# Linear-time mixers in a two-block network: three sets of block copies, a spread setup, a late norm factor and the low weights last

## The reference

```python
def rms_norm(x, g):
    y = xf * lax.rsqrt(jnp.mean(xf * xf, axis=-1, keepdims=True) + EPS)
    return (y * g.astype(jnp.float32)).astype(x.dtype)
...
def _s5_mixer(h, w_in, log_dt, lambda_re, lambda_im, b_re, b_im, c_re, c_im, d_skip, w_glu, w_out):
    u, z = jnp.split(h @ w_in, 2, axis=-1)
...
    y = jax.nn.gelu(y.reshape(bsz, seq, SSM_WIDTH)).astype(h.dtype)
    ga, gb = jnp.split(y @ w_glu, 2, axis=-1)
    y = ga * jax.nn.sigmoid(gb)
    y = y * jax.nn.silu(z)
    return y @ w_out
...
def odd_mixer(hn, w_in, w_alpha, b_alpha, out_gain, w_out):
    g_q, g_k, g_v, g_r, g_a = jnp.split(hn @ w_in, cuts, axis=-1)
    log_alpha = jax.nn.log_sigmoid((g_a @ w_alpha + b_alpha).astype(jnp.float32)) / GLA_GATE_TAU
    o = gla_chunked(to_heads(g_q, GLA_HEADS), to_heads(g_k, GLA_HEADS),
                    to_heads(g_v, GLA_HEADS), to_heads(log_alpha, GLA_HEADS))
    return (from_heads(rms_norm(o, out_gain)) * jax.nn.silu(g_r)) @ w_out
```

## Time and profile before

| | us |
|---|---|
| median of 3 timed runs | 2016.17 |
| lowest and highest | 2016.15 and 2018.51 |
| the profiled execution | 2015.85 |
| its span (first to last instruction) | 2014.1 |

### The profile page before, as it was taken

How to read it: one execution, slowest core, us unless ns; L and a number is a source line. 1 busy time by engine, 2 the same in 40 slices (tenths; PEclk the granted TensorE clock), 3 DMA queues, 4 the chain that set the end, 5 groups by cost and what they waited for, 6 DMA issues and landing times.

```text
span 2014.1 us, 26711 instructions
## 1 busy us (share of the span) xinstructions
PE 1951.5 (97%) x9866; PEld 1522.2 (76%) x9866; DVE 1121.8 (56%) x2055; ACT 582.2 (29%) x1124; POOL 799.9 (40%) x460
## 2 busy tenths in 40 slices
PE   8999999997999999999899999998999999999999
PEld 5867777776878776667678888886688778888887
DVE  5679998775974545765654445222533464454311
ACT  3136566314641134443321111001323221111100
POOL 3632222375754432222234444443233344444443
PEclk9999999998999999999999999999999999999999
DMA  5611010222212231111122222323121122222232
GB/s 183 184 63 43 33 43 33 85 65 67 69 64 94 88 127 44 62 55 61 53 96 94 94 102 96 100 99 107 53 74 63 65 94 94 99 99 94 100 119 74
DMA packets 55300, 167.66 MB, mean 83 GB/s; under 512 B 8080, under 2 KB 16144, under 8 KB 54816
## 3 DMA queue, kind: packets, MB, share of 16 engines
q1 hardware_dynamic: 47904, 155.22, 22.8%
q10 hardware_dynamic: 7296, 11.09, 2.0%
HBM read 157.90 MB, written 2.10 MB: 79 GB/s over the span
## 4 chain that ended last, share of the span: by engine, by line
issue 42%; PE 32%; POOL 17%; DVE 7%; SPq 1%; POOLq 0%; ACT 0%; DMA 0%; ACTq 0%; DVEq 0%
POOL wlo L167 16%; PE bank L184 6%; PE bank L185 6%; PE bank L186 6%; DVE prob L1620 2%; DVE ssb L1607 2%; SPq L149 1%; PE bank L1242 1%; PE bank L1267 1%; PE bank L935 1%; PE bank L554 1%; PE bank L937 1%; PE bank L936 1%; PE bank L556 1%; PE bank L555 1%
## 5 line engine op out<-in xcount | busy, mean ns | idle before, releaser
L167 POOL TENSOR_TENSOR wlo<-raw,whi 128x1024 fp32r<-128x1024 f32 x248 | 596.8, 2407 | 946.0 <-DVE whi L175 946.0
L175 DVE CAST whi<-raw 128x1024 fp32r<-128x1024 f32 x288 | 206.8, 718 | 408.7 <-PE bank L186 217.8
L184 PE MATMUL bank<-xh,whi 128*128 128x512 f32 x704 | 275.2, 391 | 3.9 <-POOL wlo L155 3.9
L185 PE MATMUL bank<-xl,whi 128*128 128x512 f32 x704 | 274.5, 390 | 0.0
L186 PE MATMUL bank<-xh,wlo 128*128 128x512 f32 x704 | 274.5, 390 | 0.0
L554 PE MATMUL bank<-xh,whi 128*128 128x512 f32 x424 | 177.6, 419 | 1.5 <-POOL wlo L167 1.5
L556 PE MATMUL bank<-xh,wlo 128*128 128x512 f32 x424 | 166.4, 392 | 0.0
L555 PE MATMUL bank<-xl,whi 128*128 128x512 f32 x424 | 165.6, 391 | 0.0
L184 PEld LDWEIGHTS bank<-xh,whi 128*128 128x128 f32 x704 | 132.5, 188 | 32.7 <-POOL wlo L155 5.2
L186 PEld LDWEIGHTS bank<-xh,wlo 128*128 128x128 f32 x704 | 132.6, 188 | 27.8
L185 PEld LDWEIGHTS bank<-xl,whi 128*128 128x128 f32 x704 | 132.6, 188 | 27.3
(11 more groups left out here) (396 smaller groups left out, 3858.9 us busy)
## 6 DMA issues: line engine op xcount, KB each, us to landing
raw<-in_weights_dram SPq DMA_DIRECT2D x288, 512.0 KB, 3.2
h<-in_x_dram SPq DMA_DIRECT2D x2, 1024.0 KB, 7.1
sz<-su SPq DMA_DIRECT2D x128, 16.0 KB, 1.8
out_dram<-h ACTq DMA_DIRECT2D x4, 512.0 KB, 2.6
etab<-in_even_tables_dram ACTq DMA_DIRECT2D x1, 1730.0 KB, 6.5
x_kh<-kvc_h ACTq DMA_DIRECT2D x2, 256.0 KB, 5.1
x_kl<-kvc_l ACTq DMA_DIRECT2D x2, 256.0 KB, 6.9
x_vh<-kvc_h ACTq DMA_DIRECT2D x2, 256.0 KB, 5.0
```

The source lines that it names most:

```text
L167: nc.gpsimd.tensor_tensor(wlo[:, s % 2, :], raw[:, s, :], whi[:, s % 2, :].bitcast(F32), ALU.subtract).then_inc(w_lo, 1)
L175: nc.vector.tensor_copy(whi[:, t_of_4 % 2, :], raw[:, t_of_4, :]).then_inc(w_hi, 1)
L184: nc.tensor.matmul(to, w_h, pe_h, start=first and k == 0, stop=False)
L185: nc.tensor.matmul(to, w_h, pe_l, start=False, stop=False)
```

## The change

It has four parts.

1. In a product tile TensorE waits for `whi` alone, does the 16 matmuls with `whi`, then waits for `wlo` and does the 8 with `wlo`. The helpers that interleave a tile with attention work in quarters (6 matmuls each) do the same in theirs. The two first tiles of each output projection (`pe_out_chunk`), the first two of `glu` and the compression loop stay in the old order.
2. The block copies of `su` are issued in three sets of 16 for the groups 0, 1 to 3 and 4 to 7, instead of eight sets: 48 DMAs instead of 128, of the same bytes in all. Tile 52 is issued behind the first set, 53 to 55 behind the second, none behind the third.
3. Pool's tables are spread over five tiles, `ta` and `tb` in turn, and it no longer fills constants: VectorE does that in six operations behind input tile 4.
4. `N_MIX1` joins `UNSCALED`: `xh` and `xl` come out of `down0`'s residual, the gates use `h` with a `wga` that VectorE scaled by the gain at the end of `up0`, and the square sums run behind the last gate. `rstd` is multiplied in by VectorE where `gas`, the values and the output gates leave their banks (ScalarE took those before) and, for queries and keys, through the exponents (`oe`, four slots instead of three). The tables are loaded at the start of `up0`.

Besides, the square sums in `nsa_kv` come one chunk earlier. The diff, cut to its core; the other product helpers change as `product` does:

```diff
-                for j in range(KC):
-                    sp_blocks(sp, j)
-                    if 2 <= j < 2 + RING:
-                        sp.wait_ge(w_lo, first + j - 2 - RING + 1)
-                        sp.dma_start(raw[:, j - 2, :], A["weights"][first + j - 2]).then_inc(w_landed[j - 2], 16)
+                for part in range(3):
+                    sp_blocks(sp, part)
+                    for slot in ((0,), (1, 2, 3), ())[part]:
+                        sp.wait_ge(w_lo, first + slot - RING + 1)
+                        sp.dma_start(raw[:, slot, :], A["weights"][first + slot]).then_inc(w_landed[slot], 16)
                 sp_tiles(sp, first // RING + 1, TILES // RING)
...
+        BLOCKS_OF = ((0, 1), (1, 4), (4, KC))
+
+        def sp_blocks(sp, part):
+
+            first, last = BLOCKS_OF[part]
+            sp.wait_ge(s_su, last)
             for q in range(4):
                 for r in range(4):
-                    sp.dma_start(sz[32 * r:32 * r + 32, j, q * P:(q + 1) * P],
-                                 su[32 * q:32 * q + 32, j, r * P:(r + 1) * P]).then_inc(s_ub[j % 4], 16)
+                    sp.dma_start(sz[32 * r:32 * r + 32, first:last, q * P:(q + 1) * P],
+                                 su[32 * q:32 * q + 32, first:last, r * P:(r + 1) * P]).then_inc(s_ub[part], 16)
 
...
-        def product(pe, par, to, rhs_hi, rhs_lo, chunks, first, last, before=None):
-
+        def product(pe, tiles, par, to, rhs_hi, rhs_lo, chunks, first, last, before=None):
+
+            w_h, w_l = ([w[:, par, k * P:(k + 1) * P] for k in range(chunks)] for w in (whi, wlo))
+            pe.wait_ge(w_hi, tiles)
             for k in range(chunks):
                 if before is not None:
                     before(k)
-                w_h, w_l = whi[:, par, k * P:(k + 1) * P], wlo[:, par, k * P:(k + 1) * P]
-                pe_h, pe_l = rhs_hi(k), rhs_lo(k)
-                nc.tensor.matmul(to, w_h, pe_h, start=first and k == 0, stop=False)
-                nc.tensor.matmul(to, w_h, pe_l, start=False, stop=False)
-                last_mm = nc.tensor.matmul(to, w_l, pe_h, start=False, stop=last and k == chunks - 1)
+                nc.tensor.matmul(to, w_h[k], rhs_hi(k), start=first and k == 0, stop=False)
+                nc.tensor.matmul(to, w_h[k], rhs_lo(k), start=False, stop=False)
+            pe.wait_ge(w_lo, tiles)
+            for k in range(chunks):
+                last_mm = nc.tensor.matmul(to, w_l[k], rhs_hi(k), start=False, stop=last and k == chunks - 1)
...
-        UNSCALED = [n for n in splitting if norms[n] in (N_S5, N_MIX0, N_FFN0, N_FFN1)]
+        UNSCALED = [n for n in splitting if norms[n] in (N_S5, N_MIX0, N_FFN0, N_MIX1, N_FFN1)]
...
+            if layer == 0:
+                for to, what in ((otab, "odd_tables"), (wga, "wga"), (walpha, "walpha"), (obias, "odd_bias")):
+                    act.dma_start(to[:], A[what]).then_inc(o_loaded, 16)
...
+            if layer == 0:
+                dve.wait_ge(o_loaded, 64)
+                nc.vector.tensor_tensor(wga[:], wga[:], gains[:, N_MIX1, :].rearrange("p (k a) -> p k a", a=1).broadcast_to([P, KC, 16]),
+                                        ALU.mult).then_inc(o_gmm, 1)
...
-            for k in (2 * quarter, 2 * quarter + 1):
-                w_h, w_l = whi[:, par, k * P:(k + 1) * P], wlo[:, par, k * P:(k + 1) * P]
+            for k in ((0, 1, 2), (3, 4, 5), (6, 7), ())[quarter]:
+                w_h = whi[:, par, k * P:(k + 1) * P]
                 nc.tensor.matmul(to[:], w_h, xh[:, k, :], start=k == 0, stop=False)
                 nc.tensor.matmul(to[:], w_h, xl[:, k, :], start=False, stop=False)
-                mm = nc.tensor.matmul(to[:], w_l, xh[:, k, :], start=False, stop=k == KC - 1)
+            if quarter == 2:
+                pe.wait_ge(w_lo, i * per + (T0[stage] + skip + r + 1))
+            for k in ((), (), (0, 1), range(2, KC))[quarter]:
+                mm = nc.tensor.matmul(to[:], wlo[:, par, k * P:(k + 1) * P], xh[:, k, :], start=False, stop=k == KC - 1)
             if quarter == 3:
...
             def gate(m):
 
-                pe.wait_ge(norm_f, SCALED[n] + m + 1)
-                nc.tensor.matmul(bank[2][0:16, :], wga[:, m, :], xf[:, m % 2, :], start=m == 0,
-                                 stop=m == KC - 1).then_inc(o_gmm, 1)
+                if m == 0:
+                    pe.wait_ge(o_gmm, 1)
+                norm_low_ready(pe, n, m)
+                mm = nc.tensor.matmul(bank[2][0:16, :], wga[:, m, :], h[:, m, :], start=m == 0, stop=m == KC - 1)
+                if m == KC - 1:
+                    mm.then_inc(o_gmm, 1)
+                    pe_squares(pe, n)
 
...
-            nc.scalar.activation(oe[:, 1, :], cum[:, i, :], ACT.Exp, scale=-1.0 / 16).then_inc(o_e, 1)
-            act.wait_ge(o_df, i + 1)
+            act.wait_ge(o_df, 3 * i + 2)
+            nc.scalar.activation(oe[:, 3, :], oe[:, 3, :], ACT.Exp, scale=1.0 / 16).then_inc(o_e, 1)
+            act.wait_ge(o_df, 3 * i + 3)
+            nc.scalar.activation(oe[:, 1, :], oe[:, 1, :], ACT.Exp, scale=-1.0 / 16).then_inc(o_e, 1)
...
+            for slot, sign in ((1, 8.0), (3, -8.0)):
+                nc.vector.scalar_tensor_tensor(oe[:, slot, :], lnv[:], sign, cum[:, i, :], ALU.mult, ALU.add).then_inc(o_df, 1)
+            dve.wait_ge(o_df, 3 * i + 1)
             nc.vector.tensor_tensor(oe[:, 2, :].rearrange("p (c t) -> p c t", t=CH),
-                                    c_i[:, :, CH - 1:CH].broadcast_to([P, NCH, CH]), c_i,
-                                    ALU.subtract).then_inc(o_df, 1)
+                                    c_i[:, :, CH - 1:CH].broadcast_to([P, NCH, CH]),
+                                    oe[:, 1, :].rearrange("p (c t) -> p c t", t=CH), ALU.subtract).then_inc(o_df, 1)
 
...
+        def dve_odd_take(dve, name, i):
+
+            dve_odd_split(dve, name, i)
+            r = odd_tile(name, i)
+            to = {"va": sq[:, 0, :], "vb": sq[:, 1, :], "ra": ogate[:, 0, :], "rb": ogate[:, 1, :]}[name]
+            nc.vector.tensor_tensor(to, acc[r % 2][:], rstd[:], ALU.mult).then_inc(acc_free[r % 2], 1)
...
             nc.vector.memset(att[:], 0.0).then_inc(o_am, 1)
-            dve_odd_split(dve, "va", 0)
+            dve.wait_ge(o_gmm, 2)
+            dve.wait_ge(rstd_ready, ORDER[N_MIX1] + 1)
+            nc.vector.tensor_tensor(gas[:], bank[2][0:16, :], rstd[0:16, :], ALU.mult).then_inc(o_ga, 1)
+            dve_odd_take(dve, "va", 0)
...
             if j == 0:
-                pool_fill(pool, xc[:], 0.0)
-            if j == 1:
                 for to in (ta, tb):
                     pool_fill(pool, to[:, 0, :, 0:1], 1.0)
                     pool_fill(pool, to[:, 1, :, 0:1], 0.0)
-                for n, m in ((1, 6), (2, 7), (4, 8)):
-                    pool_table(pool, ta, n, m)
+                pool_table(pool, ta, 1, 6)
+                pool_table(pool, tb, 1, 2)
+            if j == 1:
+                pool_table(pool, ta, 2, 7)
+                pool_table(pool, tb, 2, 3)
             if j == 2:
-                for n, m in ((1, 2), (2, 3), (4, 4)):
-                    pool_table(pool, tb, n, m)
+                pool_table(pool, ta, 4, 8)
             if j == 3:
+                pool_table(pool, tb, 4, 4)
+            if j == 4:
                 pool_table(pool, tb, 8, 5)
-            if j == 4:
-                for to, value in ((xk, 0.0), (sx[:, :, :, :, 0:1], 0.0), (kmask[:, 0:1], 0.0), (kmask[:, 1:], 1.0)):
-                    pool_fill(pool, to, value)
-                after_pool(pool)
-                nc.gpsimd.memset(xb[:], 0.0).then_inc(s_ready, 1)
 
...
+                if j == 4:
+                    for x in (xb[:], xc[:], sx[:, :, :, :, 0:1], xk, kmask[:, 0:1]):
+                        after_last(dve)
+                        nc.vector.memset(x, 0.0).then_inc(s_par, 1)
+                    dve.wait_ge(s_par, setup_steps[0])
+                    nc.vector.memset(kmask[:, 1:], 1.0).then_inc(s_ready, 1)
...
-            pool.wait_ge(s_ready, 1)
+            pool.wait_ge(n_zero, pool_steps[0])
```

145 lines of the change are left out of this document (58 added, 87 removed).

## The result

| | us |
|---|---|
| the changed kernel, median of 4 runs | 1993.16 |
| its four runs | 1998.11, 1994.61, 1980.63, 1991.72 |
| mean granted clock of these four | 0.983, 0.985, 0.995, 0.987 |
| the kernel before beside it, median of 4 | 2017.34 |
| ratio, 95% interval | 0.987 (0.9849 to 0.9891) |

The kernel is faster by 1.3%, where 2.0% was forecast, and 1993.16 lies outside the range of 1967 to 1989. The profiled execution was the slowest of the four, 1998.11 us with a span of 1996.3. The four runs spread over 17.5 us, and their order is that of the granted clock.

The account below looks back on a forecast made before the run. TensorE was taken as the bound, busy 1951.5 of 2014.1 us. Terms 1.2 + 4.4 + 7.2 + 1.5 + 15.6 + 0.7 + 8.7 = 39.3 off 2015.85 gave 1976.6, 1977 as a median; range 1967 to 1989.

Parts of the forecast that it names:

- The step that failed: Output projections' tiles 0 and 1 and the compression loop keep the old order and cost the same: 0 us.
- The sum: All terms over the whole kernel: 39.3 us saved, from 2015.85 to 1976.6 us.
- The waits on `xl`: At the odd mixer, the last chunk's xl is asked for 11 us after the last down0 matmul: covered.
- a few shifts of some tenths: Earlier first-stage square sums, gl sooner in s5_out, xf in joined square sums: both signs, set at 0.
- The S5 stage: First S5 stage: tile 53 issued 20 us sooner, second turn starts at 461.0 instead of 476.6: 15.6 us saved.
- `whi` first: Product tiles start on whi alone: nsa_kv 1.2, glu 4.4, even_out and odd_out 7.2 together, odd mixer's second pair 1.5 us saved.
- The odd mixer: Odd mixer's start: gates run at once without rstd, L1789 8.7 us sooner, 0 to 0.3 us wait for gas.
- The clock behind a wait: Behind TensorE waits of 1.9 us and more, some 3.4 us at clock 0.50, costing about 1.5 us each.
- 1: S5 stage: set 1's copies cost by size, the S5 gain of 16.3 us is gone, 1993 us; chance 0.11 above 1985.
- 3: All product tiles: the new order slows every matmul by 6.3 ns, +43.5 us, 2020 us; chance 0.04.
- 4: Product tiles: the reordering does nothing, the wlo terms of 14.3 us fall out, 1991 us; chance 0.02.
- Rival 2: Waits on wlo return at the ninth chunk or on VectorE, at S5 and four heads: 1985 to 1988 us; chance 0.10.

Follow-up runs that it names:

- e3: The changed kernel with the compression loop in the new order too: 1983.02 us, 0.9829 of the kernel before.
- e4: The changed kernel with the first tile behind each residual norm in the old order: 1981.30 us, 0.9815 of the kernel before.
- e6: The kernel before with the new order of matmuls alone, in all product helpers: 2015.39 us, ratio 0.9993.
- e12: The changed kernel with the first tile behind each residual norm in the old order and the compression loop in the new: 1980.99 us, 0.9819 of the kernel before.
- e1: The kernel before with the new order in the eight nsa_kv tiles alone, square sums there one chunk earlier: 2019.52 us, ratio 1.0019.
- e5: The changed kernel once more, unaltered: 1985.21 us, 0.9842 of the kernel before.
- e9: The kernel before with the new order in all product helpers and in the compression loop: 2009.96 us, ratio 0.9957.
- e16: e12 with the odd mixer's first tile back in the new order: 1977.04 us, 0.9804 of the kernel before.
- e11: The kernel before with one extra VectorE fill ahead of the cast for the compression loop's second tile: 2033.28 us, ratio 1.0079.
- e13: The kernel before with that extra VectorE fill (e11) and the compression loop in the new order: 2017.49 us, ratio 0.9996.
- e7: The kernel before with the copies in three sets and Pool's setup spread, nothing else: 1999.21 us, ratio 0.9908.
- e14: The kernel before with the copies in three sets alone: 2006.13 us, ratio 0.9946.
- e15: The kernel before with Pool's setup spread and the fills on VectorE alone: 2018.99 us, ratio 1.0001.
- e8: The kernel before with the odd mixer's norm factor applied late, nothing else: 2012.17 us, ratio 0.9973.
- e10: e6 with one step of VectorE's S5 coefficients moved behind the cast for the compression loop's second tile: 2022.89 us, ratio 1.0029.

## Why the prediction was wrong, point by point

**The step that failed** is the sentence that products with `pe_out_chunk` "and the compression loop keep the old order and cost what they did". The loop costs 11.1 us more in the profiled execution, and no term, rival or bound of the range stood for it. The new order shortens `nsa_kv` by 1.5 us, so the loop starts sooner, while VectorE's coefficient steps ahead of the cast for the loop's second tile keep their own time. In this profile that cast comes 1.0 us behind the loop's start instead of 0.7, and the wait on `wlo` there is 0.6 instead of 0.3 us. The other profiles bear it out: with `nsa_kv` in the old order the cast comes at 0.7 us in all six that leave VectorE's steps alone; with the new order it is at 0.8 to 1.2 in five of nine (the changed kernel, e3, e4, e6, e12) and at 0.7 in four (e1, e5, e9, e16). So the new order makes a late cast possible, not certain. That a longer wait in the loop brings half clock for 34 to 38 us is shown by e11, e13 and e9. What decides it in a single execution stays open: e4's profile has a wait of 0.6 in the loop and no stretch, the changed kernel's has the same wait and 34.1 us.

**The sum was right otherwise**, as far as a profile without the stretch shows it. Added from the table with e5, the stretches that carry a term give 1.5 + 14.9 + 1.6 + 3.7 + 3.2 + 8.7 + 1.9 + 3.5 = 39.0, against 39.3. Without the stretch the kernel takes 1983.68 in e5's profile, 7 over the 1976.6 of the sum: 4.0 stand ahead of `nsa_kv` and in the even heads, each with 6.8 us at half clock instead of 3.4, and in the sparse attention, where the 6.8 us of both profiles fall on other matmuls; 2.7 stand at `s5_out`, the even mixer's first tiles, `up0` and `up1`.

**The waits on `xl`** are most of the 2.7, and a step that I made at one place only. I found the last chunk's `xl` covered at the odd mixer, where gates lie between. Behind the four other norms TensorE now comes to it after 14 matmuls (3.2 us) instead of 21 (4.8), and waits 1.0 each. e4 gives the price, 1.3 us each, and the shift had been set at 0 under "a few shifts of some tenths".

**The S5 stage**: mechanism and size right, 14.9 of 15.6, and 0.71 us per copy within the bounds of 0.65 and 0.94. Tile 53 went out 17.6 us sooner in the stage, not 20, since the first set began 2.4 us later in it. VectorE's six fills took 3.9 us, between the 3.0 and 4.5 of the estimate. The prediction held it possible that each waits for one of Pool's operations or is stretched twofold; the two long ones ran beside Pool's and were neither (1024 elements per partition in 0.91 us, 2560 in 2.19), and no wait of TensorE came of them. The attribution was not right. I gave Pool's 3.9 us to the order of matmuls; e7 shows that the spread setup removes them without it, and e14 and e15 that the copies give 11 to 12 us alone, the spread nothing, both together 17 to 19: the second gain needs the first.

**`whi` first** at `glu`, `even_out` and `odd_out`: 3.7, 3.2 and 3.5 for 4.4, 3.9 and 3.3. What remains at `even_out` is 0.7 on `h`: the bank comes free with the residual's sum, which VectorE does behind the cast.

**The odd mixer**: 8.7 forecast, 8.7 found, and `gas` on the edge as worked out. e8 shows that this needs the eight `wlo` matmuls behind the square sums; without them 1.5 us of wait and a longer stretch at half clock take 3.4 back.

**The clock behind a wait** was read too simply. The prediction has TensorE at 0.50 for some 3.4 us "behind the waits of 1.9 us and more", but in the trace of before three waits of 1.9 us on `esp`, in the even mixer's heads, have no such stretch. Of the four waits on `esp` none is followed by one in e6's profile, in which the heads took 222.8 us, and all four in e12's, in which they took 229.2. The terms of 1.5 us of clock at `glu`, `even_out` and `odd_out` came out, but what the same wait costs in clock changes from run to run.

**Rivals**: 1 is refuted by SyncE's rows, 3 by 223 and 216 matmuls in 50 us, 4 by the waits. Rival 2 had the form of the `xl` waits, not their place or size.

## What to carry to other kernels

A change that only takes waits away still moves every engine against the others, so go through the places that are not edited as well. Here the dearest was a loop of short matmuls, where one wait of 0.4 to 0.9 us was followed by a loss of some 11 to 13 us. Running the high half first was worth it at the tile starts that waited for the low half, and not in a tile whose last chunk of input is itself late. When two edits free the same wait, test each alone and both together: here one was worth nothing alone and some 6 us beside the other.

## What the runs showed that I had not expected

A single wait inside a loop of 160-column matmuls was followed by 34.1 to 37.5 us of TensorE at a granted clock of 0.50: with 0.9 us in all five runs (e11), with 0.4 in seven of twelve (e6), with no wait in none of 31 (e3, e9, e12, e13, e16). The waits are those of one profile per kernel, the counts go by times and mean clocks. The clock fell 1.1 to 2.6 us behind the wait (the changed kernel, e6, e11) and was back at 1.00 from 1.5 to 4.8 us behind the last short matmul (these three and e10). That it is the shortness of the matmuls that keeps it down is read from this and was not tested. A fill of 32 x 384 cells, 0.38 us on VectorE, so cost 16 us.
